# Building the combining matrix of each expert block from slot numbers spread once per layer

## The chip, the cores and the metric

The kernel runs on one core of a Trainium2 chip. The metric is the device time of one execution in microseconds; the time before the change is the median of three runs, 1628.35 us (1627.49 to 1630.45).

The core has five engines that run side by side and wait for one another by semaphores: PE (TensorE: matrix products and transposes, whose results land in PSUM, 8 banks of 512 fp32 numbers for each of 128 partitions), DVE (VectorE), ACT (ScalarE), POOL (GpSimd) and SP (SyncE, which here only issues the loads of weights). Everything is computed in fp32.

## The reference, cut to what matters

Two layers run over 288 tokens of width 1024: a prompt of 256 tokens and 8 samples of 4 tokens. In each layer a token mixer (retention and a convolution) is followed by a mixture of 16 experts, each with three 1024 x 1024 matrices. Each token goes to its two best experts of one group:

```python
wts, local = lax.top_k(cand, TOP_K)            # TOP_K = 2
wts = wts / jnp.sum(wts, axis=-1, keepdims=True)
e_idx = g_sel[:, None] * EXPERTS_PER_GROUP + local
# the (token, expert) pairs are sorted by expert, padded to blocks, and for each block
#   ys = (silu(xb @ w_gate[e]) * (xb @ w_up[e])) @ w_down[e]
ys = (ys * slot_w[:, None]).astype(h.dtype)
return jnp.zeros((N + 1, D), h.dtype).at[slot_tok].add(ys)[:N]
```

## The kernel before, in words

**Weights.** All weights pass through `ring`, 12 slots of 1 MB; one expert fills it once (four slots each for gate, up and down). SP waits until a slot is free (`freed[s]`, counted up by PE, ACT and DVE after the last product that reads it) and issues its next load (line 336 for the experts).

**Routing.** After the mixer DVE works out for each token its two slot numbers `slots` and two weights `wts` (token on the partition, three tiles of 128, 128 and 32 tokens), and how many blocks of 64 slots each expert needs, `nsubi` (lines 1155 to 1232). The first block's tokens are gathered early: `sel`, a 0/1 matrix (token by slot), goes from DVE to PE, PE multiplies it with the tokens (`gather`), ACT copies the rows (`xtok`), PE transposes them, ACT copies again (`xg`). Then DVE clears `rtmp`, `selT` and `ysb`, adds a bias (line 999) and signals `route_ready`.

**Blocks.** PE, ACT and DVE run a loop over blocks. PE reads from `nsubi` how many blocks an expert has. In one block PE does, in this order: 16 half-width gate products (a product of 512 columns on the lower or the upper 64 output partitions), 16 up products, with the four pairs `combine(0..3)` of the previous block between them; `gather` for the next block; four transposes of `hs` (the gated product); three transposes of `selw` into bank 6; four transposes of the gathered rows; and 16 down products. `combine` multiplies the previous block's result `ysb` by `selT`, the weighted matrix (slot by token), and DVE adds the sums to `xT`.

`selT` comes about so: at the head of the block DVE compares `iota` (0 to 63, twice) with the slot number of each token and multiplies by its weight, for both choices (lines 1254, 1256), adds the two (1259), lowers `slots` by 64 (1260), and builds `sel` for the next block (1263, 1265, 1268). Near the end of the block PE transposes `selw`, and DVE copies `h2T` (line 1283, awaited by the down products) and then `selT` (line 1285, awaited by the next block's `combine(0)`).

**Order.** The order on each engine is the order of the program; nothing plans it at run time. PE's transposes carry line 357, its products line 354, ACT's work line 770; several DVE operations of the routing carry line 1152.

Of the kernel before, what the change touches and what calls it, by code (L numbers as in the profile page):

```python
# [10 lines left out]
NS = B * T_DEC  # L11
T = SEQ + NS
P = 128
# [30 lines left out]


CONST = [("ident", 128), ("tri", 128), ("ones", 128), ("fold", 2 * NC), ("decay", 4 * 128), ("sdecay", 4 * NS),
         ("cos", T), ("sin", T), ("qdec", 4 * (P + NS)), ("kdec", 12), ("smask", B), ("iota", 2 * BLK),
         ("ekey", E), ("gkey", GROUPS), ("valid", 3)]
COFF, _o = {}, 0
for _n, _w in CONST:  # L50
# [5 lines left out]
def constants():  # L56

    c = {}
    i = np.arange(P)
    c["ident"] = np.eye(P)  # L60
    c["tri"] = (i[:, None] < i[None, :]).astype(float)
    c["ones"] = np.ones((P, P))
    fold = np.zeros((P, 2, NC))
    for r in range(P):
        if r % 32 < NC:
            fold[r, (r // 32) % 2, r % 32] = 1.0
    c["fold"] = fold.reshape(P, -1)
    scale = DH ** -0.5
    rel = i[None, :] - i[:, None]
    c["decay"] = np.stack([np.where(rel >= 0, np.exp(np.maximum(rel, 0) * g), 0.0) * scale for g in LG], 1).reshape(P, -1)  # L70
    s = np.arange(NS)
    srel = s[None, :] - s[:, None]
    same = (s[None, :] // T_DEC == s[:, None] // T_DEC) & (srel >= 0)
    sd = np.zeros((P, 4, NS))
    for h, g in enumerate(LG):
        sd[:NS, h] = np.where(same, np.exp(np.maximum(srel, 0) * g), 0.0) * scale
    c["sdecay"] = sd.reshape(P, -1)
    half = DH // 2
    inv = (np.float32(10000.0) ** (-np.arange(half, dtype=np.float32) / np.float32(half))).astype(np.float32)
    pos = np.concatenate([np.arange(SEQ), PAST + s % T_DEC]).astype(np.float32)  # L80
    ang = (pos[None, :] * inv[:, None]).astype(np.float32).astype(np.float64)
    c["cos"] = np.concatenate([np.cos(ang), np.cos(ang)], 0)

    c["sin"] = np.concatenate([np.sin(ang), -np.sin(ang)], 0)
    qi = np.concatenate([np.arange(P) + 1, s % T_DEC + 1])
    c["qdec"] = np.broadcast_to(np.stack([np.exp(qi * g) for g in LG]).reshape(1, -1), (P, 4 * (P + NS)))
    kd = np.zeros((P, 3, 4))
    for h, g in enumerate(LG):
        kd[:, 0, h] = kd[:, 1, h] = np.exp((P - 1 - i) * g) * scale
        kd[:NS, 2, h] = np.exp((T_DEC - 1 - s % T_DEC) * g) * scale  # L90
    c["kdec"] = kd.reshape(P, -1)
    sm = np.zeros((P, B))
    sm[s, s // T_DEC] = 1.0
    c["smask"] = sm
    c["iota"] = np.broadcast_to(np.arange(2 * BLK) % BLK, (P, 2 * BLK))
    c["ekey"] = np.broadcast_to(E - np.arange(E), (P, E))
    c["gkey"] = np.broadcast_to(GROUPS - np.arange(GROUPS), (P, GROUPS))
    v = np.ones((P, 3))
    v[NS:, 2] = 0.0
    c["valid"] = v  # L100
    return np.ascontiguousarray(np.concatenate([c[n] for n, _ in CONST], 1).astype(np.float32))
# [14 lines left out]
def hybrid_step_kernel(nc, x_prompt, x_sample, state_ret, state_conv, c_prompt, c_sample, w_mod, b_mod, g_mix_norm,  # L116
# [6 lines left out]
    with ctx:  # L123
        def sb(name, shape, dt=f32):
            return ctx.enter_context(nc.sbuf_tensor(name, shape, dt))
# [16 lines left out]
        stat = sb("stat", [P, 2, T])  # L142
        rt = sb("rt", [P, 16, 3 * E])
        slot0 = sb("slot0", [P, 3])[:, :]
        wts = sb("wts", [P, 2, 3])
        slots = sb("slots", [P, 2, 3])
        nsubi = sb("nsubi", [P, E + 1], i32)
        rtmp = sb("rtmp", [P, KC, NS])
        ARENA = 14976
# [67 lines left out]
        ysb = cut("moe", 512)  # L217
        xg = cut("moe", 512)
        xtok = cut("moe", 512)
        used["moe"] = 16 * T + 2 * B * DH  # L220
        sel = cut("moe", 3, BLK)
        sel1 = cut("moe", 3, BLK)
        selw = cut("moe", 3, 2 * BLK)
        selw1 = cut("moe", 3, 2 * BLK)
        selT = cut("moe", T)
        assert used["moe"] <= cbt_start

        HEAD_BANK, SUM_BANK, VAR_BANK, OUT_BANK = (4, 5, 2, 0), (3, 7, 4, 5), (1, 2, 0, 3), (7, 4, 5, 6)
# [25 lines left out]
        snew_ready states_stored Sa_stored o_done o_copied gn_sum gn_centered gn_sq gn_var gn_mixed outproj_done x_mid  # L254
        norm2_sq norm2_sum h2_ready h2_trans h2_copied logits_done lg_ready ex_ready m_ready pos_done route_ready
        dchain pchain sel0_ready g0_done x0_copied gt0_done sel_ready gathered xrow_copied xg_trans xg_copied
        gate_done up_done sig_done gated h_act trans_done hT_copied selw_ready selT_done selT_copied
        down_done y_copied bchain comb_done0 comb_done1 comb_done2 comb_done3 comb_used0 comb_used1 comb_used2 comb_used3
        mod2_done mod2_evac mod2_fold mod2_added last_comb x_end""".split()
        S = {n: sem(n) for n in names}  # L260
# [91 lines left out]
        def _(pe):  # L352
# [3 lines left out]
            def tr(out, in_, n):  # L356
                return nc.tensor.transpose(out, in_, ident[0:n, 0:n])  # L357
# [65 lines left out]
            with pe.Fori(0, L) as l:  # L423
# [249 lines left out]
                gather().then_inc(V.g0_done, 1)  # L673
                pe.wait_ge(V.x0_copied, 1)
                transposes(1, xtok).then_inc(V.gt0_done, 1)
                pe.wait_ge(V.route_ready, 1)
                nn = pe.alloc_register("block_count")
                pe.reg_mov(nn, 0)
                with pe.Fori(0, E) as e:
                    nsub = pe.value_load(nsubi[0:1, bass.ds(e, 1)], min_val=1, max_val=MAXSUB)  # L680
                    with pe.Fori(0, nsub):
# [37 lines left out]
                        gather().then_inc(V.gathered, 1)  # L719
                        pe.wait_ge(V.h_act, nn)  # L720
                        transposes(4, hs).then_inc(V.trans_done, 1)
                        pe.wait_ge(V.selw_ready, nn)
                        for t, (t0, m) in enumerate(TILES):
                            last = tr(ps[:, 6, t0:t0 + m], selw[0:m, t, :], m)
                        last.then_inc(V.selT_done, 1)
                        pe.wait_ge(V.xrow_copied, nn)
                        transposes(1, xtok).then_inc(V.xg_trans, 1)

# [198 lines left out]
        def _(dve):  # L927
# [60 lines left out]
            with dve.Fori(0, L) as l:  # L988
# [242 lines left out]
                    tt(r3(3 + 4 * k), r3(13), r3(8 + k), ALU.mult)  # L1231
                    ch.link(v.tensor_reduce(slots[:, k, :], r3(3 + 4 * k), AX.X, ALU.add))
                v.memset(rtmp[:, :, :], 0.0)
                v.memset(selT, 0.0).then_inc(V.selT_copied, 1)
                dve.wait_ge(V.mod2_fold, 2)
                add_mod_bias(7, 0, 5).then_inc(V.route_ready, 1)
                dve.wait_ge(V.route_ready, 1)
                dve.sem_inc(routed, 1)
                dve.wait_ge(V.states_stored, 32)
                v.memset(ysb, 0.0).then_inc(V.y_copied, 1)  # L1240
                dve.wait_ge(V.g0_done, 1)

                def take(j):
# [6 lines left out]

                nb = dve.value_load(nsubi[0:1, E:E + 1], min_val=E, max_val=MAXBLK)
                with dve.Fori(0, nb) as n:
                    for t in range(3):
                        v.tensor_scalar(selw[:, t, :], iota, slots[:, 0, t:t + 1], wts[:, 0, t:t + 1], ALU.is_equal, ALU.mult)  # L1254
                    for t in range(3):
                        last = v.tensor_scalar(selw1[:, t, :], iota, slots[:, 1, t:t + 1], wts[:, 1, t:t + 1], ALU.is_equal, ALU.mult)
                    last.then_inc(V.bchain, 1)
                    dve.wait_ge(V.bchain, n * 3 + 1)
                    v.tensor_tensor(selw[:, :, :], selw[:, :, :], selw1[:, :, :], ALU.add).then_inc(V.selw_ready, 1)
                    v.tensor_scalar(slots[:, :, :], slots[:, :, :], -float(BLK), None, ALU.add).then_inc(V.bchain, 1)  # L1260
                    dve.wait_ge(V.bchain, n * 3 + 2)
                    for t in range(3):
                        v.tensor_scalar(sel[:, t, :], iota[:, 0:BLK], slots[:, 0, t:t + 1], None, ALU.is_equal)
                    for t in range(3):
                        last = v.tensor_scalar(sel1[:, t, :], iota[:, 0:BLK], slots[:, 1, t:t + 1], None, ALU.is_equal)
                    last.then_inc(V.bchain, 1)
                    dve.wait_ge(V.bchain, n * 3 + 3)
                    v.tensor_tensor(sel[:, :, :], sel[:, :, :], sel1[:, :, :], ALU.add).then_inc(V.sel_ready, 1)

                    for j in range(2):  # L1270
# [10 lines left out]
                    v.tensor_tensor(hs, ps[:, 3, :], hs, ALU.mult).then_inc(V.h_act, 1)  # L1281
                    dve.wait_ge(V.trans_done, n + 1)
                    v.tensor_copy(h2T, ps[:, 4, :]).then_inc(V.hT_copied, 1)  # L1283
                    dve.wait_ge(V.selT_done, n + 1)
                    v.tensor_copy(selT, ps[:, 6, 0:T]).then_inc(V.selT_copied, 1)

                dve.drain()
                racc = rtmp[:, :, :].rearrange("p k (b t) -> p k b t", b=B)
# [140 lines left out]
```

## Time and profile before

| what | value |
|---|---|
| median of 3 runs | 1628.35 us (1627.49 to 1630.45) |
| the profiled execution's own time | 1627.57 us |
| its span | 1626.0 us |
| PE busy | 1512.6 us, 93% |
| DVE busy | 673.5 us, 41% |
| ACT busy | 234.3 us, 14% |
| POOL busy | 105.7 us, 6% |
| weights read from HBM and other reads | 495.32 MB |
| the chain that ended last | PE 64%, DVE 14%, SP's queue 14%, DMA 4% |

The span runs from the first to the last instruction of the profiled execution. Busy time is summed over the instructions of an engine without counting overlap twice. The chain that ended last is followed back from the last instruction, at each step to what released it. A row with an L number belongs to that line of the kernel; "x11" is the number of instructions merged in a row. An fp32 product or a transpose of a full tile leaves one or two matmul records.

### The profile page before, as it was taken

How to read it: one execution, taken by the hardware profiler on the slowest of the kernel's cores; microseconds unless marked ns; L12 is line 12 of the kernel's file. 1: busy time of each engine (PE TensorE's matmuls, PEld its weight loads, DVE VectorE, ACT ScalarE, POOL GpSimd, SP SyncE). 2: the span in 40 equal slices, each digit the busy share in tenths (PEclk: the TensorE clock that was granted, in tenths of full speed). 3: DMA queues.
4: the chain of work that ended last, by engine and by line, in shares of the span. 5: the costliest groups of instructions: out<-in, count | busy, mean ns of one | idle time of the engine just before them, and what ended most of it. 6: DMA issues, size and time to landing. Idle time of an engine off the chain costs nothing.

```text
span 1626.0 us, 19889 instructions
## 1 busy us (share of the span) xinstructions
PE 1512.6 (93%) x7061; PEld 698.9 (43%) x7062; DVE 673.5 (41%) x1953; ACT 234.3 (14%) x371; POOL 105.7 (6%) x146
## 2 busy tenths in 40 slices
PE   5779899899999999999995998989999999999996
PEld 3157677533333333333334776763333332333333
DVE  0027934643334333333432694454333333333333
ACT  2011121111111111111111012111111111111112
POOL 0007100200000000000000620020000000000000
PEclk9679979799999999999997997888999999999998
DMA  9973530979999998499993244086999999989990
GB/s 348 403 295 123 192 136 1 374 289 411 410 410 410 410 410 312 160 399 410 410 410 145 104 161 186 1 344 251 407 410 410 410 410 410 407 312 410 410 410 37
DMA packets 132129, 501.97 MB, mean 309 GB/s; under 512 B 9647, under 2 KB 10071, under 8 KB 131950
## 3 DMA queue, kind: packets, MB, share of 16 engines
q1 hardware_dynamic: 127036, 487.97, 76.2%
q0 software_dynamic: 3392, 11.01, 1.9%
q10 hardware_dynamic: 1666, 2.53, 0.5%
q8 instruction: 22, 0.36, 0.1%
q14 instruction: 13, 0.11, 0.0%
HBM read 495.32 MB, written 7.00 MB: 309 GB/s over the span
## 4 chain that ended last, share of the span: by engine, by line
PE 64%; DVE 14%; SPq 14%; DMA 4%; issue 2%; ACT 1%; PEldq 0%; POOLq 0%; PEld 0%; DVEq 0%; ACTq 0%
PE ps L354 60%; SPq L336 11%; DVE arena L1030 7%; PE ps L357 4%; DMA ring<-in_w_exp_up 2%; SPq L303 2%; DMA ring<-in_w_mod 1%; DVE arena L960 1%; DVE hT L966 1%; DMA arena<-in_w_conv 1%; DVE hT L971 1%; ACT arena L770 1%; DVE stat L960 0%; PEldq L752 0%; DVE arena L1042 0%
## 5 line engine op out<-in xcount | busy, mean ns | idle before, releaser
L354 PE MATMUL ps<-ring,arena 128*64 128x512 f32 x3360 | 765.6, 600 | 6.7 <-DMA ring<-in_w_exp_gate 2.9
L354 PEld LDWEIGHTS ps<-ring,arena 128*64 128x64 f32 x3360 | 224.8, 137 | 452.1 <-issue 421.8
L1246 DVE SCALAR_TENSOR_TENSOR xT<-ps,mod,xT 128x256 f32<-128x256 f32 x280 | 134.0, 478 | 414.6 <-PE ps L354 414.6
L354 PE MATMUL ps<-arena 64*128 64x288 f32 (+6 forms) x1276 | 278.5, 499 | 22.8 <-DVE arena L1042 12.6
L354 PE MATMUL ps<-hT,ring 128*128 128x288 f32 x1024 | 258.1, 415 | 18.5 <-DVE hT L971 18.1
L770 ACT ACTIVATE arena<-ps 128x512 f32<-128x512 f32 (+3 forms) x242 | 132.0, 552 | 971.5 <-PE ps L354 802.8
L354 PEld LDWEIGHTS ps<-hT,ring 128*128 128x128 f32 x1024 | 198.8, 195 | 76.6 <-issue 18.7
L354 PEld LDWEIGHTS ps<-arena 64*128 64x128 f32 (+5 forms) x1276 | 117.9, 183 | 227.3 <-issue 201.6
L1030 DVE SCALAR_TENSOR_TENSOR arena<-arena,wc 128x256 f32<-128x256 f32 x240 | 118.5, 571 | 0.0
L770 ACT ACT_TABLE_LOAD x49 | 62.9, 1283 | 303.3 <-PE ps L354 287.5
L357 PE MATMUL ps<-cst,arena 128*128 128x128 f32 (+5 forms) x501 | 78.1, 290 | 27.7 <-DVE arena L940 12.8
L357 PEld LDWEIGHTS ps<-cst,arena 128*128 128x128 f32 (+5 forms) x501 | 56.1, 144 | 72.7 <-issue 62.2
L354 PE MATMUL ps<-ring,condT 128*32 128x512 f32 x384 | 57.7, 725 | 9.6 <-DMA ring<-in_w_mod 9.5
L1283 DVE COPY arena<-ps 128x512 f32<-128x512 f32 x35 | 24.2, 692 | 87.2 <-PE ps L357 87.2
L1274 DVE TENSOR_TENSOR arena<-ps,arena 128x512 f32<-128x512 f32 x35 | 24.2, 692 | 67.6 <-ACT arena L770 67.6
L1248 DVE TENSOR_TENSOR rtmp<-ps,rtmp 128x32 f32<-128x32 f32 x280 | 50.6, 181 | 0.0
L1281 DVE TENSOR_TENSOR arena<-ps,arena 128x512 f32<-128x512 f32 x35 | 24.2, 692 | 61.9 <-PE ps L354 61.9
L1353 POOL TENSOR_TENSOR arena<-arena,wc 128x128 f32<-128x128 f32 x62 | 32.8, 561 | 145.9 <-DVE arena L1016 145.5
L1326 POOL DMA_DIRECT2D out<-in_state_conv x2 | 1.1, 544 | 569.1 <-issue 538.9
L354 PE MATMUL ps<-arena,cst 128*128 128x288 f32 x80 | 29.3, 506 | 1.6 <-DVE xT L986 1.6
L354 PEld LDWEIGHTS ps<-ring,condT 128*32 128x32 f32 x384 | 11.1, 120 | 45.5 <-DMA ring<-in_w_mod 27.0
L1254 DVE TENSOR_SCALAR arena<-cst,slots,wts 128x128 f32<-128x128 f32 x105 | 29.8, 340 | 1.3 <-issue 1.3
(146 smaller groups left out, 621.7 us busy)
## 6 DMA issues: line engine op xcount, KB each, us to landing
ring<-in_w_exp_gate SPq DMA_DIRECT2D x128, 1024.0 KB, 14.7
ring<-in_w_exp_up SPq DMA_DIRECT2D x128, 1024.0 KB, 16.2
ring<-in_w_exp_down SPq DMA_DIRECT2D x128, 1024.0 KB, 15.4
ring<-in_w_mod SPq DMA_DIRECT2D x48, 1024.0 KB, 13.2
ring<-in_w_in SPq DMA_DIRECT2D x24, 1024.0 KB, 18.3
ring<-in_w_out SPq DMA_DIRECT2D x8, 1024.0 KB, 7.7
big<-in_state_ret POOLq DMA_DIRECT2D x4, 512.0 KB, 10.5
arena<-in_state_ret POOLq DMA_DIRECT2D x4, 512.0 KB, 10.1
```

The costliest lines, as they stand in the source:

```text
L303: sp.dma_start(ring[:, s], mod_v[bass.ds(l, 1), q, :, :, j * D:(j + 1) * D] .rearrange("a p k c -> (a p) k c")).then_inc(loaded[s], 16)
L336: sp.dma_start(ring[:, s], exp_v[j][bass.ds(l * E + e, 1), q] .rearrange("a p k c -> (a p) k c")).then_inc(loaded[s], 16)
L354: return nc.tensor.matmul(out, lhsT, rhs, start=start, stop=stop, skip_group_check=True)
L357: return nc.tensor.transpose(out, in_, ident[0:n, 0:n])
L770: return nc.scalar.activation(out, in_, f, **kw)
L1030: ins = v.scalar_tensor_tensor(cT[:, ct, 0:SEQ], src, wcol, cT[:, ct, 0:SEQ], ALU.mult, ALU.add)
L1246: v.scalar_tensor_tensor(xT[:, c, 0:SEQ], ps[:, bank, 0:SEQ], mod[:, M_GT2 + c, 0:1], xT[:, c, 0:SEQ], ALU.mult, ALU.add)
L1248: last = v.tensor_tensor(rtmp[:, c, :], ps[:, bank, SEQ:T], rtmp[:, c, :], ALU.add)
L1254: v.tensor_scalar(selw[:, t, :], iota, slots[:, 0, t:t + 1], wts[:, 0, t:t + 1], ALU.is_equal, ALU.mult)
L1274: v.tensor_tensor(hs, ps[:, 2, :], gs, ALU.mult).then_inc(V.gated, 1)
L1281: v.tensor_tensor(hs, ps[:, 3, :], hs, ALU.mult).then_inc(V.h_act, 1)
L1353: last = gp.tensor_tensor(slot[:, k].rearrange("p c (b t) -> p c b t", b=B), win[:, :, :, tap:tap + T_DEC], wc[:, tap * CT:(tap + 1) * CT] ...
```

## The change

The constant `iota` shrinks to 64 columns, and a column `pid` (partition number modulo 64) is added. `slots` and `wts` become one tile `routes`. Once per layer DVE builds `diag`: for each token tile and each of the four routing columns the identity times that column. PE multiplies it by the all-ones matrix, so that each partition holds the slot numbers and weights of all tokens, and DVE copies this into `spread`. PE waits for these three copies (`spread_copied`) ahead of the block loop. In each block the seven operations for `selw`, its three transposes and the copy of `selT` go, and DVE builds `selT` from `spread` by comparing with `pid`, which it raises by 64 per block.

```diff
+        routes = sb("routes", [P, 4, 3])
+        slots, wts = routes[:, 0:2, :], routes[:, 2:4, :]
+        spread = cut("moe", 4, T)
+        diag = arena[:, 3 * D:3 * D + 3 * 512].rearrange("p (t c) -> p t c", t=3)
 # PE, once per layer, behind the first block's transposes
                 transposes(1, xtok).then_inc(V.gt0_done, 1)
+                pe.wait_ge(V.diag_ready, 1)
+                pe.wait_ge(V.snew_ready, 4)
+                for t, (t0, m) in enumerate(TILES):
+                    last = mm(ps[:, 2 + t, 0:4 * m], ones[0:m, :], diag[0:m, t, 0:4 * m], True, True)
+                last.then_inc(V.spread_done, 1)
+                pe.wait_ge(V.spread_copied, 3)
                 pe.wait_ge(V.route_ready, 1)
 # PE, in each block
                         transposes(4, hs).then_inc(V.trans_done, 1)
-                        pe.wait_ge(V.selw_ready, nn)
-                        for t, (t0, m) in enumerate(TILES):
-                            last = tr(ps[:, 6, t0:t0 + m], selw[0:m, t, :], m)
-                        last.then_inc(V.selT_done, 1)
                         pe.wait_ge(V.xrow_copied, nn)
 # DVE, once per layer
                 v.memset(rtmp[:, :, :], 0.0)
-                v.memset(selT, 0.0).then_inc(V.selT_copied, 1)
+                for t, (t0, m) in enumerate(TILES):
+                    last = v.tensor_tensor(diag[0:m, t, 0:4 * m].rearrange("p (a c) -> p a c", a=4),
+                                           bc(ident[0:m, 0:m], 4), bl(routes[0:m, :, t], m), ALU.mult)
+                last.then_inc(V.diag_ready, 1)
+                v.tensor_copy(pid[:, :], C("pid"))
                 dve.wait_ge(V.mod2_fold, 2)
                 add_mod_bias(7, 0, 5).then_inc(V.route_ready, 1)
                 dve.wait_ge(V.route_ready, 1)
                 dve.sem_inc(routed, 1)
                 dve.wait_ge(V.states_stored, 32)
+                v.memset(selT, 0.0).then_inc(V.selT_copied, 1)
                 v.memset(ysb, 0.0).then_inc(V.y_copied, 1)
+                dve.wait_ge(V.spread_done, 1)
+                for t, (t0, m) in enumerate(TILES):
+                    v.tensor_copy(spread[:, :, t0:t0 + m], ps[:, 2 + t, 0:4 * m].rearrange("p (a c) -> p a c", a=4)) \
+                        .then_inc(V.spread_copied, 1)
 # DVE, in each block
-                    for t in range(3):
-                        v.tensor_scalar(selw[:, t, :], iota, slots[:, 0, t:t + 1], wts[:, 0, t:t + 1], ALU.is_equal, ALU.mult)
-                    for t in range(3):
-                        last = v.tensor_scalar(selw1[:, t, :], iota, slots[:, 1, t:t + 1], wts[:, 1, t:t + 1], ALU.is_equal, ALU.mult)
-                    last.then_inc(V.bchain, 1)
-                    dve.wait_ge(V.bchain, n * 3 + 1)
-                    v.tensor_tensor(selw[:, :, :], selw[:, :, :], selw1[:, :, :], ALU.add).then_inc(V.selw_ready, 1)
...
                     v.tensor_copy(h2T, ps[:, 4, :]).then_inc(V.hT_copied, 1)
-                    dve.wait_ge(V.selT_done, n + 1)
-                    v.tensor_copy(selT, ps[:, 6, 0:T]).then_inc(V.selT_copied, 1)
+                    for k, dst in enumerate((selT, selT1)):
+                        last = v.scalar_tensor_tensor(dst, spread[:, k, :], pid[:, 0:1], spread[:, 2 + k, :], ALU.is_equal, ALU.mult)
+                    last.then_inc(V.bchain, 1)
+                    dve.wait_ge(V.bchain, n * 4 + 3)
+                    v.tensor_tensor(selT, selT, selT1, ALU.add).then_inc(V.selT_copied, 1)
+                    v.tensor_scalar(pid[:, :], pid[:, :], float(BLK), None, ALU.add).then_inc(V.bchain, 1)
+                    dve.wait_ge(V.bchain, n * 4 + 4)
```

## Rows read from the trace of the kernel before

**Rows 1.** Chain of waits, in order of time: start, duration, what.

```profile
583.73 18.16 DMA ring<-in_w_exp_up
...
1392.96 18.37 DMA ring<-in_w_exp_up
```

**Rows 2.** Timeline of PE, the transposes of six blocks: start, duration, engine, line.

```profile
550.16 1.63 PE L357 MATMUL ps<-cst,arena 128*128 128x128 f32 x11
578.54 1.63 PE L357 MATMUL ps<-cst,arena 128*128 128x128 f32 x11
609.09 1.64 PE L357 MATMUL ps<-cst,arena 128*128 128x128 f32 x11
...
836.14 1.63 PE L357 MATMUL ps<-cst,arena 128*128 128x128 f32 x11
...
1418.53 1.63 PE L357 MATMUL ps<-cst,arena 128*128 128x128 f32 x11
...
1588.82 1.63 PE L357 MATMUL ps<-cst,arena 128*128 128x128 f32 x11
```

**Rows 3.** Timeline, all engines, end of one block: in brackets idle before, and releaser.

```profile
408.25 1.63 PE L357 MATMUL ps<-cst,arena 128*128 128x128 f32 x11
408.37 0.60 ACT L770 ACTIVATE arena<-ps 128x512 f32<-128x512 f32 x1 [9.30 <-PE ps L354]
408.94 0.69 DVE L1283 COPY arena<-ps 128x512 f32<-128x512 f32 x1 [2.49 <-PE ps L357]
...
409.81 0.20 PEld L354 LDWEIGHTS ps<-ring,arena 128*64 128x64 f32 x4 [0.17 <-DVE arena L1283]
...
409.92 0.60 ACT L770 ACTIVATE arena<-ps 128x512 f32<-128x512 f32 x1 [0.96 <-PE ps L357]
...
413.35 0.36 DVE L1268 TENSOR_TENSOR arena<-arena 128x192 f32<-128x192 f32 x1
...
420.27 0.76 PE L354 MATMUL ps<-arena 64*128 64x288 f32 x4
```

**Rows 4.** Groups of DVE by line and shape: busy, mean ns of one.

```profile
L1069 DVE SCALAR_TENSOR_TENSOR arena<-arena,vec,hT 128x288 f32<-128x288 f32 x8 | 3.6, 512 | 0.4 <-ACT hT L770 0.4
...
L1100 DVE TENSOR_TENSOR arena<-arena 128x288 f32<-128x288 f32 x8 | 3.3, 409 | 0.0
...
L1077 DVE SCALAR_TENSOR_TENSOR arena<-arena,ps 128x128 f32<-128x128 f32 x8 | 1.8, 282 | 0.1
```

**Rows 5.** Timeline ahead of the first block, layer 0.

```profile
327.23 0.27 DVE L1233 MEMSET rtmp<- 128x256 f32 x1
...
328.37 0.66 PE L357 MATMUL ps<-cst,arena 128*128 128x128 f32 x4 [0.76 <-ACT arena L770]
329.06 0.60 ACT L770 ACTIVATE arena<-ps 128x512 f32<-128x512 f32 x1 [0.75 <-PE ps L357]
...
329.91 5.27 PE L354 MATMUL ps<-ring,arena 128*64 128x512 f32 x16 [0.89 <-ACT arena L770]
```

**Rows 6.** Timeline ahead of the first block, layer 1.

```profile
1089.60 3.69 PE L354 MATMUL ps<-arena 32*128 32x512 f32 x8 [0.76 <-ACT arena L770]
...
1103.78 0.27 DVE L1233 MEMSET rtmp<- 128x256 f32 x1
...
1105.88 1.11 PE L357 MATMUL ps<-cst,arena 128*128 128x128 f32 x4 [0.76 <-ACT arena L770]
...
1107.83 4.57 PE L354 MATMUL ps<-ring,arena 128*64 128x512 f32 x12 [0.83 <-ACT arena L770]
```

**Rows 7.** Windows: length, busy us of PE, PEld, DVE, ACT, POOL, granted clock, DMA share, GB/s.

```profile
326.40:329.80 3.40, 1.86 (x10) 0.61 (x8) 2.41 (x10) 1.19 (x2) 0.00 (x0) 1.00 0.00 0
329.80:333.20 3.40, 3.29 (x8) 1.03 (x10) 3.04 (x13) 0.00 (x0) 0.00 (x0) 0.50 0.00 0
...
1108.00:1111.40 3.40, 3.40 (x10) 0.94 (x12) 1.73 (x9) 0.00 (x0) 0.00 (x0) 0.50 0.00 0
1111.40:1114.80 3.40, 3.40 (x20) 1.06 (x18) 0.80 (x3) 0.00 (x0) 0.00 (x0) 0.99 0.55 136
```

More of the change, by code:

```diff
@@ L46 @@
 CONST = [("ident", 128), ("tri", 128), ("ones", 128), ("fold", 2 * NC), ("decay", 4 * 128), ("sdecay", 4 * NS),
-         ("cos", T), ("sin", T), ("qdec", 4 * (P + NS)), ("kdec", 12), ("smask", B), ("iota", 2 * BLK),
+         ("cos", T), ("sin", T), ("qdec", 4 * (P + NS)), ("kdec", 12), ("smask", B), ("iota", BLK), ("pid", 1),
          ("ekey", E), ("gkey", GROUPS), ("valid", 3)]
@@ L94, in constants @@
     c["smask"] = sm
-    c["iota"] = np.broadcast_to(np.arange(2 * BLK) % BLK, (P, 2 * BLK))
+    c["iota"] = np.broadcast_to(np.arange(BLK), (P, BLK))
+    c["pid"] = (i % BLK)[:, None]
     c["ekey"] = np.broadcast_to(E - np.arange(E), (P, E))
@@ L144, in hybrid_step_kernel @@
         slot0 = sb("slot0", [P, 3])[:, :]
-        wts = sb("wts", [P, 2, 3])
-        slots = sb("slots", [P, 2, 3])
+        routes = sb("routes", [P, 4, 3])
+        slots, wts = routes[:, 0:2, :], routes[:, 2:4, :]
+        pid = sb("pid", [P, 1])
         nsubi = sb("nsubi", [P, E + 1], i32)
@@ L219, in hybrid_step_kernel @@
         xtok = cut("moe", 512)
-        used["moe"] = 16 * T + 2 * B * DH
+        selT = cut("moe", T)
+        selT1 = cut("moe", T)
         sel = cut("moe", 3, BLK)
         sel1 = cut("moe", 3, BLK)
-        selw = cut("moe", 3, 2 * BLK)
-        selw1 = cut("moe", 3, 2 * BLK)
-        selT = cut("moe", T)
+        spread = cut("moe", 4, T)
+        diag = arena[:, 3 * D:3 * D + 3 * 512].rearrange("p (t c) -> p t c", t=3)
         assert used["moe"] <= cbt_start
@@ L256, in hybrid_step_kernel @@
         dchain pchain sel0_ready g0_done x0_copied gt0_done sel_ready gathered xrow_copied xg_trans xg_copied
-        gate_done up_done sig_done gated h_act trans_done hT_copied selw_ready selT_done selT_copied
+        gate_done up_done sig_done gated h_act trans_done hT_copied diag_ready spread_done spread_copied selT_copied
         down_done y_copied bchain comb_done0 comb_done1 comb_done2 comb_done3 comb_used0 comb_used1 comb_used2 comb_used3
@@ L1252, in _ @@
                 with dve.Fori(0, nb) as n:
-                    for t in range(3):
-                        v.tensor_scalar(selw[:, t, :], iota, slots[:, 0, t:t + 1], wts[:, 0, t:t + 1], ALU.is_equal, ALU.mult)
-                    for t in range(3):
-                        last = v.tensor_scalar(selw1[:, t, :], iota, slots[:, 1, t:t + 1], wts[:, 1, t:t + 1], ALU.is_equal, ALU.mult)
-                    last.then_inc(V.bchain, 1)
-                    dve.wait_ge(V.bchain, n * 3 + 1)
-                    v.tensor_tensor(selw[:, :, :], selw[:, :, :], selw1[:, :, :], ALU.add).then_inc(V.selw_ready, 1)
-                    v.tensor_scalar(slots[:, :, :], slots[:, :, :], -float(BLK), None, ALU.add).then_inc(V.bchain, 1)
-                    dve.wait_ge(V.bchain, n * 3 + 2)
+                    v.tensor_scalar(slots, slots, -float(BLK), None, ALU.add).then_inc(V.bchain, 1)
+                    dve.wait_ge(V.bchain, n * 4 + 1)
                     for t in range(3):
@@ L1266, in _ @@
                     last.then_inc(V.bchain, 1)
-                    dve.wait_ge(V.bchain, n * 3 + 3)
+                    dve.wait_ge(V.bchain, n * 4 + 2)
                     v.tensor_tensor(sel[:, :, :], sel[:, :, :], sel1[:, :, :], ALU.add).then_inc(V.sel_ready, 1)
```

## The prediction

> **What bounds the kernel now.** I read the chain of waits first. In the expert stage it runs for the most part through PE, block after block, but it passes once in each layer through a load of weights [rows 1]. So the stage has two limits, and I looked next for where each holds. PE's timeline gives the period: the train of 11 transposes near a block's end comes at 550.16 and 578.54, which is 28.38 us [rows 2]. One train later the distance is 30.55 us, because the weights were late by 2.17 us. From 609.09 to 836.14 lie 8 periods of 28.38 us without a stall, and in layer 1 six from 1418.53 to 1588.82. The reader is to see that time saved in a block counts only behind the last late load: earlier blocks wait for the weights anyway, and a faster PE would wait longer. Behind it lie 9 passages from transposes to down products in layer 0 (609.09 to 836.14, both ends counted) and 7 in layer 1, so 16 of the 35 blocks.
>
> Then the block's end in detail [rows 3]. The 11 transposes start at 408.25 and the down products load their first weights at 409.81, so a transpose takes 1.56 / 11 = 0.142 us of the train. The down products also need DVE's copy of `h2T`, which runs from 408.94 to 409.63 and starts when the first four transposes are through. The three transposes of `selw` lie beside this copy.
>
> Last, the start of the stage [rows 5, 6]. PE starts the first gate product as soon as ACT's second copy is there: the copy ends at 329.66 in layer 0, the product starts at 329.91, and in layer 1 it starts at 1107.83. The DMA share is 0.00 just before and for some us after this [rows 7]: the ring is full, and the loads of the next expert wait for slots that only the first block frees. A delay of the first block thus moves both limits, PE and the weight stream, and nothing behind it takes it back.
>
> **The change, part by part.**
>
> *Three transposes less in each block.* They took 3 x 0.142 = 0.43 us of PE. What is late next is the copy of `h2T`: its trigger, the four transposes of `hs`, does not move, and it ends at 409.63. Beside it the four transposes of gathered rows wait for ACT's copy, which ends at 408.97; 4 x 0.142 on top gives 409.54. So the down products, now at 409.81, could start at 409.63 at the earliest. The gain is between 0 and 0.18 us a block; PE now starts 0.18 us after this copy, and 0.25 us after ACT's in rows 5; a part of the 0.18 is the hand-over and stays, so I take 0.07. Times 16 blocks that is 1.1 us, with ends 0 and 2.9.
>
> *DVE's work in each block.* Seven operations and the copy of `selT` go. Behind the `h2T` copy come two operations like L1069, 0.51 us each, one like L1100, 0.41 us [rows 4], and one on a single column, below 0.28 us (the 128-column row). `selT` is then ready about 1.5 us behind 409.63, near 411.1, and PE wants it for `combine(0)` at 420.27 [rows 3]: 9 us of cover. `sel` for the next gather follows in the place where it stood before (complete at 413.71, wanted at the next block's end, some 20 us later). Cost nothing; only if DVE grew by more than 9 us would it count. ACT's copy into `xg` comes up to 0.4 us earlier than 409.92, with 7 us of down products before anyone reads it: nothing.
>
> *The spread, once per layer.* This is new on the path, since PE waits for it ahead of its first gate product. Its steps:
> - DVE multiplies three times for `diag`: 0.69 us twice for 512 columns (the 512-column copy of rows 3 is the nearest) and 0.28 us for 128 columns (rows 4). They start where `rtmp` is cleared, at 327.50 and 1104.05, and end at 329.16 and 1105.71. PE's transposes end at 329.03 and 1106.99, so in layer 0 the matrix is 0.1 us late and in layer 1 it is covered. The bias, `route_ready` and the two clearings come 1.8 us later on DVE; they lie beside PE's products.
> - PE multiplies by ones: 512, 512 and 128 columns at full width. The nearest row is 8 records in 3.69 us for four such products at full clock, 0.92 us each [rows 6]; at the lower clock twice that, 1.84. The sum is 2.07 us at full and 4.14 us at the lower clock. In layer 0 the clock was full until 329.80 and then the lower level [rows 7], so from 329.2: 0.6 us are 65% of the first, the rest 0.64, then 1.84 and 0.46, end 332.75. In layer 1 all lies at the lower level: 1107.05 to 1111.2.
> - DVE copies three banks out, and its first copy waits for the last product: 0.69 + 0.69 + 0.28 = 1.66 us, with 0.1 us for two hand-overs. PE goes on at 334.5 and 1112.95.
> - PE then reads the block count into a register. Before, this lay beside ACT's copy. It took no more than the 0.88 us from 329.03 to 329.91, and at least 0; I take 0.4, as no row parts it from the wait.
>
> So the first gate product starts at 334.9 instead of 329.91 and at 1113.3 instead of 1107.83: 5.0 + 5.5 = 10.5 us. Bounds: with the products at full clock, copies overlapped by 0.1 each and a free register read it is 3.0 + 2.8 = 5.8; with the whole 0.88 twice it is 11.5. What was queued behind the new wait is the whole block loop of PE, and through it ACT, DVE and SP's loads.
>
> *The clock behind the spread.* The first block started at the lower of the two levels, 1.2 GHz, and the full 2.4 GHz came at 333.2 and 1111.4, after PE had been busy with products for 3.3 and 3.6 us [rows 5, 7]. Half of that was lost, 1.7 and 1.8 us. Now the spread products come just ahead; the clock may be full when the first gate product starts, which gives back all of it, or may fall again because PE idles for some 2 us while DVE copies (it fell at 329.8 after a stretch in which PE was busy for 1.86 of 3.4 us). Between -1.8 and +0.7 us a layer (the ramp then starts in the middle of the block); I take -0.7, so -1.4 in all.
>
> *A rule of the skill.* Rows 2 price the work that goes, 0.43 us a block beside other work, and rows 6 the work that comes, about 4 us a layer on the path. The Trainium skill, Perfetto Trace Analysis, section Transposes, says that a logical transpose should stay a transpose, since a transpose skips the arithmetic of a product. The change goes the other way, and by that rule it should pay only if one spread is cheaper than the layer's transposes. By the rows all transposes of a layer's 17 or 18 blocks are 7.7 us of PE, and the spread is 4.1; the rule alone would call the change a gain of some 7 us for both layers. What it leaves out is that those transposes were covered and the spread isn't.
>
> *The rest.* `iota` is 63 columns shorter in the first load: nothing.
>
> **The sum.** On the profiled execution's own 1627.57 us: +10.5 - 1.4 - 1.1 = +8.0, so 1635.6. That execution is 0.8 us below the median of the runs, so I predict 1628.35 + 8.0 = 1636.3 us.
>
> **The rivals.**
> - *The transposes were on the path.* Then a block shrinks by the full 0.43 us, but only in the 16 blocks behind the late loads: -6.9 instead of -1.1, time 1630.6. For it: the chain runs through the train, and the gap in front of the down products is 0.17 us only. Against: the copy ends at 409.63 whatever PE leaves out. Chance 0.10.
> - *The other side: the weight stream does not hold the early blocks.* Its stalls are short, and if the loads keep up with a faster PE all 35 blocks gain 0.43 us: -15.1 + 10.5 - 1.4 = -6.0, time 1622.4. It decides from 24 blocks on (10.5 / 0.43). Against: the waits for `w_exp_up` are there in both layers. It needs the copy not to bind as well. Chance 0.07.
> - *The clock falls in the gap.* The first block of each layer ramps in its middle: +1.4 instead of -1.4, time 1639.1. For it: the fall at 329.8 after a thin stretch. Against: the spread is two full-width products, denser than the half-width ones. Chance 0.15. The Trainium skill, TensorE: Matmul & The Clock Gate, section "Why this matters for your kernels", asks for no idle gaps between bursts of products; by that rule this case would be the one.
> - *A cheap start.* The clock is full during the spread too: 5.8 - 1.4 - 1.1 = +3.3, time 1631.6. Chance 0.06.
>
> **How the numbers follow.** 0.62 stays for the forecast. About 0.2% or 3.3 us is what a measurement of this kernel can tell from no change, so slower begins at 1631.6. Slower: the forecast without a tail of 0.02, the clock case, half of the cheap start, 0.78 in all. Same: the first rival, the other half and that tail, 0.14. Faster: 0.08. The low end of the range is just below the first rival, 1630.5; the high end is 11.5 + 1.4 - 0 = +12.9, 1641.2. That leaves the case of a gain outside.
>
> **What would show it.** The trains of transposes (8 instead of 11) come 28.25 to 28.38 us apart where no load is late. If they come 27.95 apart, the copy did not bind. The first gate product starts 4.5 to 6 us later against the last route operation in both layers, behind three DVE copies. The weight stream at 410 GB/s stays, and so do late loads in the middle of each layer. The forecast is wrong if the first block starts less than 3 us later, or if blocks ahead of the late loads shorten the layer.

## The result, and the profile after

The changed kernel takes 1639.26 us (median of 4 runs, 1638.30 to 1642.83) against 1628.34 us before. The ratio is 1.0066, with a 95% interval from 1.0051 to 1.0081: slower by 10.9 us. Predicted were 1636.3 us. The profiled execution took 1639.92 us, with a span of 1638.2 us.

| per execution | before | after |
|---|---|---|
| span, us | 1626.0 | 1638.2 |
| PE busy, us | 1512.6 | 1511.7 |
| DVE busy, us | 673.5 | 644.2 |
| instructions | 19889 | 19616 |
| first gate product behind the clearing of `rtmp`, layers 0 and 1, us | 2.68, 4.05 | 10.45, 7.30 |

All engines are busy for less time, and the kernel is slower. The last line says where: the chain is longer ahead of the first block.

This is the timeline of the changed kernel ahead of layer 0's first block, the answer to [rows 5]; columns as there. L1239 builds `diag`, L1252 copies the spread out.

```profile
328.04 0.27 DVE L1237 MEMSET rtmp<- 128x256 f32 x1
328.22 1.41 DVE L1239 TENSOR_TENSOR arena<-cst,routes 128x512 f32<-128x512 f32 x3
...
330.14 1.11 PE L359 MATMUL ps<-cst,arena 128*128 128x128 f32 x4 [0.76 <-ACT arena L774]
...
331.05 4.34 PE L356 MATMUL ps<-arena,cst 128*128 128x512 f32 x6
331.30 0.60 ACT L774 ACTIVATE arena<-ps 128x512 f32<-128x512 f32 x1 [1.21 <-PE ps L359]
...
335.43 1.49 DVE L1252 COPY arena<-ps 128x512 f32<-128x512 f32 x3 [4.51 <-PE ps L356]
...
338.49 5.35 PE L356 MATMUL ps<-ring,arena 128*64 128x512 f32 x16 [3.10 <-issue]
```

And layer 1, the answer to [rows 6]:

```profile
1113.34 0.27 DVE L1237 MEMSET rtmp<- 128x256 f32 x1
...
1115.45 2.30 PE L356 MATMUL ps<-arena,cst 128*128 128x512 f32 x6
...
1117.78 1.49 DVE L1252 COPY arena<-ps 128x512 f32<-128x512 f32 x3 [1.57 <-PE ps L356]
...
1120.64 5.21 PE L356 MATMUL ps<-ring,arena 128*64 128x512 f32 x16 [2.89 <-issue]
```

Three pieces follow one another: the products by ones (4.34 us at the lower clock, 2.30 at the full one), the copies (1.49), and a gap from the last copy's end to the first gate product, 336.92 to 338.49 and 1119.27 to 1120.64, so 1.57 and 1.37 us. The releaser "issue" on the last row says that nothing the profile shows ended this gap.

The windows of the changed kernel show the clock there (seventh figure; columns as in [rows 7]), first layer 0, then layer 1:

```profile
331.90:335.40 3.50, 3.50 (x6) 1.17 (x4) 0.00 (x0) 0.00 (x0) 0.00 (x0) 0.51 0.00 0
335.40:338.80 3.40, 0.31 (x2) 0.20 (x4) 2.99 (x11) 0.00 (x0) 0.00 (x0) 0.99 0.00 0
338.80:342.30 3.50, 3.50 (x10) 1.03 (x8) 0.00 (x0) 0.00 (x0) 0.00 (x0) 0.52 0.00 0
342.30:345.70 3.40, 3.40 (x18) 1.08 (x16) 1.07 (x4) 0.00 (x0) 0.00 (x0) 1.00 0.68 206
...
1113.70:1117.20 3.50, 2.74 (x12) 1.07 (x8) 2.22 (x7) 1.19 (x2) 0.00 (x0) 1.00 0.00 0
1117.20:1120.30 3.10, 0.55 (x3) 0.29 (x2) 2.48 (x10) 0.00 (x0) 0.00 (x0) 1.00 0.00 0
1120.30:1123.60 3.30, 2.96 (x8) 1.02 (x10) 0.51 (x2) 0.00 (x0) 0.00 (x0) 0.52 0.00 0
```

In layer 0 the clock rises as the spread products end; in layer 1 it is full already when they begin. In both layers PE then idles for some 3 us with the full clock granted (0.31 of 3.40 us busy in layer 0), and the first gate products run at the lower level of 1.2 GHz. The block pays the ramp, the stretch at the lower level until the clock is full, as it did before the change.

The end of a block, the answer to [rows 3]:

```profile
388.40 1.42 PE L359 MATMUL ps<-cst,arena 128*128 128x128 f32 x8
388.52 0.60 ACT L774 ACTIVATE arena<-ps 128x512 f32<-128x512 f32 x1 [9.30 <-PE ps L356]
389.10 0.69 DVE L1289 COPY arena<-ps 128x512 f32<-128x512 f32 x1 [2.48 <-PE ps L359]
389.17 0.42 PEld L359 LDWEIGHTS ps<-cst,arena 128*128 128x128 f32 x4 [0.34 <-ACT arena L774]
389.70 0.94 DVE L1291 SCALAR_TENSOR_TENSOR arena<-arena,pid 128x288 f32<-128x288 f32 x2
389.84 0.20 PEld L356 LDWEIGHTS ps<-ring,arena 128*64 128x64 f32 x4 [0.26 <-DVE arena L1289]
```

There are eight transposes instead of eleven, and from their start to the down products it is 1.44 us instead of 1.56. The copy of `h2T` (L1289) ends at 389.79, and the weights of the down products are loaded 0.05 us later: the copy is what PE waits for.

The `h2T` copies also give the period. This is DVE's timeline, here on both sides of the late loads and at the ends of the stage (the answer to [rows 2]; a copy starts 0.7 us behind its train):

```profile
558.65 0.69 DVE L1289 COPY arena<-ps 128x512 f32<-128x512 f32 x1 [2.49 <-PE ps L359]
587.87 0.69 DVE L1289 COPY arena<-ps 128x512 f32<-128x512 f32 x1 [2.49 <-PE ps L359]
618.59 0.69 DVE L1289 COPY arena<-ps 128x512 f32<-128x512 f32 x1 [2.49 <-PE ps L359]
...
844.65 0.69 DVE L1289 COPY arena<-ps 128x512 f32<-128x512 f32 x1 [2.49 <-PE ps L359]
...
1340.65 0.69 DVE L1289 COPY arena<-ps 128x512 f32<-128x512 f32 x1 [2.49 <-PE ps L359]
1370.78 0.69 DVE L1289 COPY arena<-ps 128x512 f32<-128x512 f32 x1 [2.49 <-PE ps L359]
...
1432.22 0.69 DVE L1289 COPY arena<-ps 128x512 f32<-128x512 f32 x1 [2.49 <-PE ps L359]
1601.77 0.69 DVE L1289 COPY arena<-ps 128x512 f32<-128x512 f32 x1 [2.49 <-PE ps L359]
```

From 618.59 to 844.65 are 8 periods of 28.26 us, from 1432.22 to 1601.77 six of them. The late loads cost more than before: 29.22 + 30.72 - 2 x 28.26 = 3.42 us in layer 0 (before 2.17), and in layer 1, from 1340.65 over three periods, 91.57 - 3 x 28.26 = 6.79 us (before, by the same sum over its own periods of 28.85 and twice 30.72, 5.15). What the earlier blocks gained went back there: from the first `h2T` copy to the last late one it is 257.75 us in layer 0 (before 257.60) and 289.38 in layer 1 (before 288.96).

### The profile page after: what moved, and what is told of

It is laid out like the page before. It is cut to its first block, busy times and chain, and to the rows that moved or that the text cites. A ratio compares the mean times of both kernels' runs of the same rounds, so it can differ in the third digit from the quotient of the medians.

```text
span 1638.2 us, 19616 instructions
## 1 busy us (share of the span) xinstructions
PE 1511.7 (92%) x6968; PEld 693.4 (42%) x6969; DVE 644.2 (39%) x1827; ACT 233.8 (14%) x371; POOL 105.6 (6%) x146
## 4 chain that ended last, share of the span: by engine, by line
PE 60%; SPq 16%; DVE 13%; DMA 4%; issue 3%; ACT 2%; PEldq 1%; POOLq 0%; PEld 0%; DVEq 0%; ACTq 0%
PE ps L356 57%; SPq L338 14%; DVE arena L1034 7%; PE ps L359 3%; DMA ring<-in_w_exp_up 2%; SPq L305 2%; ACT arena L774 2%; DMA ring<-in_w_mod 1%; DVE arena L964 1%; DMA arena<-in_w_conv 1%; DVE hT L970 1%; DVE hT L975 1%; PEldq L756 0%; DVE arena L1045 0%; DVE arena L1046 0%
## 5 line engine op out<-in xcount | busy, mean ns | idle before, releaser
L359 PE MATMUL ps<-cst,arena 128*128 128x128 f32 (+5 forms) x396 | 67.3, 299 | 32.7 <-DVE arena L944 12.8
L359 PEld LDWEIGHTS ps<-cst,arena 128*128 128x128 f32 (+5 forms) x396 | 44.4, 148 | 78.9 <-issue 56.4
L356 PE MATMUL ps<-ring,condT 128*32 128x512 f32 x384 | 53.8, 686 | 9.3 <-DMA ring<-in_w_mod 9.1
L1289 DVE COPY arena<-ps 128x512 f32<-128x512 f32 x35 | 24.2, 692 | 87.2 <-PE ps L359 87.2
L356 PE MATMUL ps<-arena,cst 128*128 128x288 f32 (+2 forms) x92 | 36.0, 530 | 1.7 <-DVE xT L990 1.7
L1291 DVE SCALAR_TENSOR_TENSOR arena<-arena,pid 128x288 f32<-128x288 f32 x70 | 32.8, 511 | 0.0
## 6 DMA issues: line engine op xcount, KB each, us to landing
arena<-in_state_ret POOLq DMA_DIRECT2D x4, 512.0 KB, 11.1
```

Of the source, the lines that this page charges most:

```text
L356: return nc.tensor.matmul(out, lhsT, rhs, start=start, stop=stop, skip_group_check=True)
L1291: last = v.scalar_tensor_tensor(dst, spread[:, k, :], pid[:, 0:1], spread[:, 2 + k, :], ALU.is_equal, ALU.mult)
```

## The experiments

Each was timed in alternation with the kernel before. Executions of one and the same kernel lay up to 14 us apart in these comparisons, so an interval is some 2 to 4 us to each side, and the traces carry the finer points.

| run | ratio to before | 95% interval |
|---|---|---|
| e1, spread only | 1.0052 | 1.0032 to 1.0073 |
| e2, blocks only | 0.9989 | 0.9969 to 1.0008 |
| e3, wait in the loop | 1.0028 | 1.0012 to 1.0043 |
| e4, free banks | 1.0005 | 0.9988 to 1.0021 |
| e5, changed kernel again | 1.0054 | 1.0033 to 1.0074 |
| e6, e4 and reordered block | 0.9980 | 0.9966 to 0.9994 |
| e7, before with light loads | 0.9932 | 0.9912 to 0.9952 |
| e8, e2 with light loads | 0.9914 | 0.9893 to 0.9935 |
| e9, filled gap | 1.0052 | 1.0033 to 1.0072 |
| e10, e3 again | 1.0061 | 1.0040 to 1.0082 |

**e1 and e2: the two halves of the change.** e1 adds to the kernel before:

```diff
+                for t, (t0, m) in enumerate(TILES):
+                    last = mm(ps[:, 2 + t, 0:4 * m], ones[0:m, :], diag[0:m, t, 0:4 * m], True, True)
+                last.then_inc(V.spread_done, 1)
+                pe.wait_ge(V.spread_copied, 3)
```

with `diag` and the copies on DVE. e2 takes the same lines out of the changed kernel:

```diff
-                pe.wait_ge(V.spread_copied, 3)
...
+                v.memset(spread[:, :, :], 0.0).then_inc(V.spread_copied, 1)
```

> The kernel before, with the once-per-layer spread added (diag on DVE, three products by ones, three copies, PE waits for them) and the blocks left as they were; nothing reads the spread. Theory (the loss is the start of the expert stage): about +12 us against before, that is the +10.9 of the whole change plus the 1 to 2 us that its blocks give back. Rival (a part of the loss comes from the blocks, for instance DVE's new operations): clearly less, +8 or below.

> The changed kernel with the diag products, the products by ones, their copies and PE's wait left out; DVE clears the spread instead, so the combining matrix is zero and the output lacks the experts' part. Theory (a block is 0.12 us shorter, but only the 16 blocks behind the late loads count): -1.9 us against before, period 28.26 us, and the late loads wait longer by what the earlier blocks gained. Rival (the weight stream doesn't hold the early blocks): 35 x 0.12 = -4.2 us.

Measured: e1 1637.07 us, e2 1626.67 us, before 1629.15 us. By the ratios that is +8.5 and -1.8 us. The whole change, timed again as e5, had +8.8 us. So the loss is the start's, and DVE's new work in the blocks costs nothing. The 8.5 lies nearer to the rival's 8 than to my 12, but its interval runs from 5.2 to 11.9, so the time alone does not part them. e1's trace does: its period stays 28.38 us, and its first `h2T` copies come 29.6 and 32.6 us behind the clearing of `rtmp`, against 24.95 and 26.48 before, together +10.8 us. The changed kernel has 32.80 and 29.50, together +10.9. e2 keeps 28.26 us and has late loads as the changed kernel (29.57 and 30.72 us for the two periods up to 609.91, by its `h2T` copies). Of the 35 x 0.12 = 4.2 us only 1.6 came out between the first and the last `h2T` copies of the two layers; the time agrees with -1.8, but its interval (-5.0 to +1.3) would allow 4.2 too.

**e7 and e8: the weight stream.** Both load half of each down matrix, and the products use old weights for the other half:

```diff
-                            sp.dma_start(ring[:, s], exp_v[j][bass.ds(l * E + e, 1), q]
+                            sp.dma_start(ring[:, s, 0:1] if j == 2 else ring[:, s],
+                                         (exp_v[j][bass.ds(l * E + e, 1), q, :, 0:1] if j == 2 else exp_v[j][bass.ds(l * E + e, 1), q])
```

> The kernel before, with only half of each down matrix loaded (the other half of its slot keeps old weights, so the experts' part of the output is not the reference's). Theory (weights are late by 2.2 us in layer 0 and 5.2 us in layer 1 and nowhere else): -7.3 us against before, all periods 28.38. Rival (the waits for loads are not what holds PE there): less than 2 us.

> The changed blocks without the spread (combining matrix zero, the experts' part missing from the output), with the same half down loads. Theory (with no late load every block keeps its 0.12 us): -4.2 us against the run before with light loads, -11.5 against before, all periods 28.26. Rival (the blocks ahead of the late loads lose their gain to something else): -1.9 against the light run before.

Measured: 1616.43 and 1613.36 us against 1628.22, by the ratios -11.1 and -14.0 us. e7 fell by more than the 7.3 us of the late loads (the interval's near end is 7.8 us). In its profiled execution, 12.4 us shorter than the one before, 7.3 lie between the first and the last `h2T` copies of the two layers. The other 5.1 lie outside them, and what they are stays open. Between e7 and e8 lie 2.9 us by the ratios, where 4.2 were expected; their intervals overlap, so the times alone don't tell 4.2 from 1.9. The `h2T` copies in the traces do. First e7, then e8, at the place of the late loads:

```profile
580.28 0.69 DVE L1284 COPY arena<-ps 128x512 f32<-128x512 f32 x1 [2.49 <-PE ps L358]
608.66 0.69 DVE L1284 COPY arena<-ps 128x512 f32<-128x512 f32 x1 [2.49 <-PE ps L358]
637.04 0.69 DVE L1284 COPY arena<-ps 128x512 f32<-128x512 f32 x1 [2.49 <-PE ps L358]
```

```profile
579.83 0.69 DVE L1278 COPY arena<-ps 128x512 f32<-128x512 f32 x1 [2.49 <-PE ps L360]
608.09 0.69 DVE L1278 COPY arena<-ps 128x512 f32<-128x512 f32 x1 [2.49 <-PE ps L360]
636.35 0.69 DVE L1278 COPY arena<-ps 128x512 f32<-128x512 f32 x1 [2.49 <-PE ps L360]
```

All periods of both layers are 28.38 us in e7 and 28.26 in e8; no block is late. From the first to the last `h2T` copies e8 is 4.1 us shorter than e7, so now all blocks keep their gain. It is the weight stream that holds the middle of each layer.

**e3 and e10: the read of the block count.** PE's wait for the copies moves behind the read and into the loops:

```diff
-                pe.wait_ge(V.spread_copied, 3)
                 pe.wait_ge(V.route_ready, 1)
...
+                        pe.wait_ge(V.spread_copied, 3)
                         pe.wait_ge(V.xg_copied, nn)
```

> The changed kernel, only PE's wait for the three copies moved from ahead of the block loop into it, just before the gate products, behind the read of the block count. Theory (the 1.4 to 1.5 us between the last copy's end and the first gate product are the read of the block count and the entry of two loops, which now lie beside the copies of 1.5 us): the gap falls to 0.1 to 0.3 us in each layer, -2.6 us against the changed kernel, +8.3 against before. Rival (the gap is PE starting again after a wait, whatever comes before it): no change, +10.9.

> The kernel with PE's wait for the copies inside the block loop, again, beside the one with the filled gap. Its gap closed by 1.2 us in each layer, which accounts for 2.4 of the 5.6 us by which its median lay closer to before than that of the changed kernel. Theory (the rest was chance of the clock in these executions): the two calls together come to about +7. Rival (a shorter gap also spares ramps): +4.6 again.

The gap closed. This is e3's timeline, layer 0; the copies end at 338.93 and the gate products start 0.21 us later (0.19 in layer 1), where the changed kernel took 1.57:

```profile
337.44 1.49 DVE L1252 COPY arena<-ps 128x512 f32<-128x512 f32 x3 [3.47 <-PE ps L356]
...
339.14 5.35 PE L356 MATMUL ps<-ring,arena 128*64 128x512 f32 x16 [1.74 <-DVE arena L1252]
```

The gap was therefore PE's way from the wait through the read of the count and into two loops, 1.2 to 1.4 us (the runs don't part the read from the loops); a plain restart after a wait takes 0.2. The times don't show this gain. They are 1633.68 against 1629.15, then 1638.73 against 1628.61, ratios 1.0028 and 1.0061, so +4.6 and +9.9 us, and the first interval (+2.0 to +7.0) leaves out the 8.3 expected. Their mean of 7.2 is what the expectation of e10 gave for both together, and "a shorter gap spares ramps" is not borne out. e10's trace shows how much an execution can lose to the clock: it ran the products by ones and the first gate products of both layers at 0.50 (the windows of its start, layer 0 and then layer 1):

```profile
331.00:335.00 4.00, 4.00 (x7) 1.36 (x5) 0.00 (x0) 0.60 (x1) 0.00 (x0) 0.50 0.00 0
337.00:342.00 5.00, 5.00 (x12) 1.44 (x14) 1.25 (x7) 0.00 (x0) 0.00 (x0) 0.50 0.05 4
1116.00:1120.00 4.00, 4.00 (x8) 1.46 (x6) 0.00 (x0) 0.60 (x1) 0.00 (x0) 0.50 0.00 0
1122.00:1127.00 5.00, 4.88 (x12) 1.49 (x14) 1.43 (x7) 0.00 (x0) 0.00 (x0) 0.50 0.00 0
```

**e4: no wait for the copies.** The products by ones go to banks that the block uses only later. DVE clears `ysb` behind its copies, and `combine(0)`, which waits for that, can't overwrite a bank before it is copied:

```diff
+        SPREAD_BANK = (6, 7, 5)
...
-                pe.wait_ge(V.snew_ready, 4)
+                pe.wait_ge(V.route_ready, 1)
...
-                pe.wait_ge(V.spread_copied, 3)
-                pe.wait_ge(V.route_ready, 1)
... on DVE, behind the copies:
+                dve.wait_ge(V.spread_copied, 3)
+                v.memset(ysb, 0.0).then_inc(V.y_copied, 1)
```

> The changed kernel with the spread products in banks 6, 7 and 5, which the block needs only from its first combine on, so that PE does not wait for the copies at all; the clearing of ysb behind the copies keeps the order. Theory: the copies (1.5 us), the exposed read (1.4 us) and the clock's fall in that gap go, the products stay; with the clock's ramp lying in the products the start costs about 2 us a layer, in all +4.2 - 1.9 = +2.3 us against before. Rival (the clock plays no part and only waits go): 10.9 - 2 x 2.9 = +5 us. Rival (only the copies go, the read stays exposed behind the products): about +8 us.

Measured 1630.84 against 1629.15, +0.8 us by the ratio (-2.0 to +3.4). Of the three theories the first, with the clock in it, fits (+2.3); +5 and +8 are outside. By the trace the first `h2T` copies come 25.02 and 28.12 us behind the clearing, together +1.7. e4's timeline, layer 0, has gate products right behind the spread's, and its windows, layer 0 and layer 1, are at the full clock or close to it:

```profile
333.35 2.30 PE L357 MATMUL ps<-arena,cst 128*128 128x512 f32 x6
335.58 3.65 PE L357 MATMUL ps<-ring,arena 128*64 128x512 f32 x16
335.69 1.49 DVE L1250 COPY arena<-ps 128x512 f32<-128x512 f32 x3 [2.14 <-PE ps L357]
```

```profile
335.60:339.00 3.40, 3.40 (x17) 1.04 (x16) 2.66 (x9) 0.00 (x0) 0.00 (x0) 1.00 0.05 11
...
1116.20:1120.00 3.80, 3.80 (x19) 1.17 (x18) 3.27 (x12) 0.00 (x0) 0.00 (x0) 0.95 0.16 24
```

The 16 records of the first gate products took 3.65 us, 5.27 before the change [rows 5]. The spread products cost 2.3 us in layer 0 and 4.3 in layer 1 here, and spare the block a ramp of 1.6 to 1.7 us each time.

**e9: the clock by itself.** Three more products by ones fill PE's gap:

```diff
                 last.then_inc(V.spread_done, 1)
+                for _ in range(3):
+                    mm(ps[:, 6, :], ones, diag[:, 0, :], True, True)
                 pe.wait_ge(V.spread_copied, 3)
```

> The changed kernel with three more products by ones (512 columns, into bank 6, read by nobody) behind the spread products, so that PE has work while DVE copies and while the block count is read. Theory (the clock, raised by the spread products, falls again in the gap of some 3 us and the first block pays a second ramp): the first gate product starts no later than before, 1.4 to 1.6 us behind the last copy, the granted clock is full through the first block, -1.7 us a layer, -3.4 against the changed kernel, about +6 against before. Rival (the clock's fall has another reason): the ramp stays, and the time is that of the changed kernel or above, +9 to +11.

The trace agrees with the theory: the gate products start 1.58 and 1.38 us behind the last copy, as in the changed kernel, and from the filling products on the clock is full (windows of layer 0 and of layer 1):

```profile
336.00:340.00 4.00, 3.88 (x10) 1.35 (x8) 2.79 (x11) 0.00 (x0) 0.00 (x0) 1.00 0.00 0
340.00:344.00 4.00, 3.79 (x18) 1.31 (x20) 0.20 (x1) 0.00 (x0) 0.00 (x0) 1.00 0.19 20
...
1121.00:1124.00 3.00, 2.92 (x8) 1.10 (x10) 2.89 (x11) 0.00 (x0) 0.00 (x0) 1.00 0.00 0
1124.00:1128.00 4.00, 4.00 (x20) 1.20 (x16) 0.00 (x0) 0.00 (x0) 0.00 (x0) 1.00 0.21 35
```

From the first gate product to the first `h2T` copy it is 20.64 us in both layers, against 22.35 and 22.20 in the changed kernel: the ramps of 1.7 and 1.6 us are gone. So idling caused the second ramp. But the time did not follow: 1638.27 against 1628.61, ratio 1.0052, so +8.5 us (+5.4 to +11.7) where I expected about +6; the interval holds both. In its profiled execution the stretches behind the first gate products are 3.3 us shorter than in the changed kernel's, but these products start 9.46 and 10.26 us behind the clearing, together 2.0 later, since the clock was at the lower level ahead of the spread and in most of it. That hides a good part of what the ramps gave. Whether filling the gap pays on average stays open.

**e5: the changed kernel again.**

> The changed kernel itself, timed beside the others of this call, since executions of one kernel lay up to 14 us apart in the last comparison. Theory (its loss is the start of the stage, two exposed waits and two clock ramps): +8 to +11 us against before. Rival (a part of the first +10.9 was chance of which ramp an execution met): +5 us or less, like the kernel with the wait in the loop.

Measured 1638.43 (1631.20 to 1642.91) against 1628.22: +8.8 us by the ratio. So the first +10.9 was not chance, as the theory said. In its trace the first `h2T` copies come 29.55 and 31.27 us behind the clearing, together +9.4 us.

**e6: what the freed PE time could give.** On top of e4:

```diff
-                        gather().then_inc(V.gathered, 1)
+                        gather((0, 1))
                         pe.wait_ge(V.h_act, nn)
                         transposes(4, hs).then_inc(V.trans_done, 1)
-                        pe.wait_ge(V.xrow_copied, nn)
-                        transposes(1, xtok).then_inc(V.xg_trans, 1)
+                        gather((2,)).then_inc(V.gathered, 1)
... in the down products:
+                            if k == 3:
+                                pe.wait_ge(V.xrow_copied, nn)
+                                transposes(1, xtok).then_inc(V.xg_trans, 1)
... on DVE, at the block's end:
+                    dve.wait_ge(V.gathered, n + 1)
```

> The kernel with free banks, and in each block the last two gather products moved behind the transposes of hs and the transposes of the gathered rows moved into the down products (behind the fourth pair), so that PE has work while DVE copies h2T. Theory (since the change the h2T copy is what holds a block's end: 0.42 us of PE work were freed and only 0.12 came out): the period falls from 28.26 to 27.9 to 28.0 us, 16 x 0.3 = -4.9 us against the kernel with free banks, about 1625 where before is 1629. Rival (switching between transposes and products costs PE what the cover gives): period stays at 28.2 or grows, no gain.

Measured 1625.58 against 1628.22, ratio 0.9980 (0.9966 to 0.9994): the only version that leaves nothing out and is faster than the kernel before, by about 3 us. Its timeline:

```profile
384.05 0.66 PE L360 MATMUL ps<-cst,arena 128*128 128x128 f32 x4
384.64 0.19 PEld L357 LDWEIGHTS ps<-arena 32*64 32x64 f32 x4 [0.17 <-issue]
384.64 1.07 PE L357 MATMUL ps<-arena 32*64 32x512 f32 x4
384.75 0.69 DVE L1292 COPY arena<-ps 128x512 f32<-128x512 f32 x1 [1.48 <-PE ps L360]
```

The copy now lies beside the last gather products. The period is 28.14 to 28.15 us, not 27.9 to 28.0: of 0.3 us 0.11 came out, between theory and rival. Why the rest is missing was not tried; the added switches between transposes and products are a possible reason, not a shown one. From the first to the last `h2T` copies the two layers are 3.5 us shorter than in e4's trace. Only 1.6 of them lie behind the last late loads; the rest lies ahead of them, about 1 us a layer, where a limit by the weight stream alone would let nothing out. Why is not shown.

## Why the prediction was right, and where its sizes were off

The direction and the place were right, and the time was 3 us above the forecast. That the parts add up so nearly is partly luck, as the first items show.

- *The start is on the path and nothing takes it back.* Right: e1 shows the loss alone, and e4 takes nearly all of it away. Predicted were +5.0 and +5.5 us for the first gate product, 4.5 to 6 in each layer; the trace has +7.8 and +3.2. Neither lies in that span, and the second is just above the 3 us below which the forecast was to count as wrong. The sum is 11.0 for 10.5 because its errors cancel: over both layers the read took 2.1 us more than reckoned, the copies with their hand-overs 0.5 less, and the clock gave 1.2 back. In layer 0 the gather and the transposes ran at the lower level where before it was the full one, so the spread began 3.01 us behind the clearing, not 1.97. In layer 1 it was the other way round, 2.11 for 3.27. Other executions met other levels and came to like sums, +11.0 in e1 and +10.0 in e5.
- *The read of the block count* is the term that was mis-sized: I took 0.4 us and kept 0.88 as its upper bound. It measured 1.57 and 1.37 us from the last copy, 1.2 to 1.4 more than with the wait behind it (e3). The bound was wrong because I counted it from the transposes' end. A way of 1.2 to 1.4 us doesn't fit into 0.88, so before the change PE's sequencer must have begun it while the transposes were still running; that is worked out, and no row shows the moment.
- *The spread products* were right in price and not in clock: 4.34 and 2.30 us for 3.55 and 4.14. Which level they meet changed from execution to execution. The three `diag` operations (1.41 us for 1.66) and the three copies (1.49 for 1.66) overlap by some 0.1 us from one to the next.
- *The clock behind the spread* was taken at -0.7 us a layer; it gave 0. From the gate start to the first `h2T` copy it is 22.35 and 22.20 us, before 22.27 and 22.43. The rival "the clock falls in the gap" came true in its mechanism: the clock was full by the end of the spread, PE idled for 3.1 and 2.9 us, and about when it went on the clock fell. The Trainium skill's rule against idle gaps between bursts (TensorE: Matmul & The Clock Gate, "Why this matters for your kernels") agrees with this trace and with e9. The rival's price of +0.7 us a layer was too high in this execution. In e10 the same stretch took 23.3 us in both layers, +1.1 and +0.8, but there the clock had not risen on the spread at all.
- *Three transposes less* gave 0.12 us a block, within the bounds of 0 and 0.18 and above the 0.07 taken; the copy of `h2T` binds, as argued. From first to last `h2T` copy the two layers gained 0.9 and 0.3 us, 1.2 for the 1.1 predicted. Here too two errors cancel: the 14 periods behind the late loads gained 1.7 us, and the stretches up to the last late copies grew by 0.6, which no run explains.
- *The weight stream holds the middle of each layer.* Right, by e7 and e8 (e6 shows that a reordered block can still gain some there). The rival in which all 35 blocks count is out, and so is the one with 0.43 us a block.
- *DVE's work is covered.* Right: `selT` comes from work that ends within 2 us of the copy of `h2T`, and no period grew.
- The spans differ by 12.2 us; the stage explains 10.9 - 1.2 = 9.7. The other 2.5 lie outside it, where the program is unchanged: 0.8 ahead of the first stage and 1.7 between the layers, where for instance the same 16 records of the sum of squares took 5.84 us instead of 4.15.

## What to carry to other kernels

Work that leaves an engine on the path counts only up to the next wait beside it, and only where no other limit holds; here 0.43 us a block shrank to 0.12, and 35 blocks to about 15. Work put ahead of a loop counts in full when nobody is ahead of it, and a wait ahead of a loop also exposes what the sequencer used to do early, register reads and loop entry. Put such a wait as late as its buffers allow (here this closed the gap in the trace, and the times did not settle what it is worth), or choose buffers that need none (here this took back nearly the whole loss). When a change frees an engine's time beside a wait, reorder so that other work covers the wait, or the gain stays inside.

## What the runs showed of the hardware

- Reading a count into a register and entering two loops kept PE's first product back by 1.2 to 1.4 us after a wait, with nothing in the profile but "issue" (the changed kernel); the same wait behind them left 0.2 us (e3).
- In the changed kernel the granted clock was full by the end of the spread products, stayed full while PE idled for some 3 us, and was at the lower level about when the products came back (0.99, then 0.52 in the windows above; with the gap filled, e9, 1.00 throughout). The full clock of the idle stretch said nothing about the work behind it.
- The same 6 records of the spread took 4.34 us and 2.30 us in the two layers of one execution, by the level of the clock. Executions of one program spread over 14 us in these comparisons; the level at the start of the stages, which varies between the traces, accounts for a few of them, and the rest is open.
